# Unread products of a tile of ones at the ends and starts of the linear stages

## The reference, cut to what matters

```
def _rmsnorm(x, g):
    xf = x.astype(jnp.float32)
    y = xf * lax.rsqrt(jnp.mean(xf * xf, axis=-1, keepdims=True) + EPS)
    return (y * g.astype(jnp.float32)).astype(x.dtype)
...
        proj = _rmsnorm(h, norm_mix_g[l]) @ w_in[l]
...
        h = h + mixed @ w_out[l]
        h = h + _memory_attention(_rmsnorm(h, norm_mem_g[l]), ...)
        h = h + _peer_ffn(_rmsnorm(h, norm_peer_g[l]), ...)
...
    xn = rmsnorm(x, norm1_g)
    proj = xn @ w_in
...
    mixed = g_ssd * (y_ssd @ w_ssd_out) + g_mla * (y_mla @ w_mla_out) + g_gdn * (y_gdn @ w_gdn_out)
    h = x + mixed @ w_out
    f = jnp.square(jax.nn.relu(rmsnorm(h, norm2_g) @ w_up)) @ w_down
```

## Time and profile before

| | us |
|---|---|
| median of three timed runs | 5384.28 |
| lowest and highest of them | 5381.77, 5384.46 |
| profiled execution | 5380.81 |
| its span, first to last instruction | 5379.00 |
| PE busy in it | 5036.6 (94%) |
| DVE busy | 3028.1 (56%) |
| ACT busy | 1726.1 (32%) |
| POOL busy | 704.4 (13%) |
| mean granted TensorE clock | 0.959 |

### The profile page before, as it was taken

How to read it: one execution, slowest core, us unless ns; L and a number is a source line. 1 busy time by engine, 2 the same in 40 slices (tenths; PEclk the granted TensorE clock), 3 DMA queues, 4 the chain that set the end, 5 groups by cost and what they waited for, 6 DMA issues and landing times. The chain is left out here.

```text
span 5379.0 us, 61794 instructions
## 1 busy us (share of the span) xinstructions
PE 5036.6 (94%) x23862; PEld 4037.5 (75%) x23862; DVE 3028.1 (56%) x5431; ACT 1726.1 (32%) x2636; POOL 704.4 (13%) x493
## 2 busy tenths in 40 slices
PE   8778899999999999988899998999998999989998
PEld 6237678888878888877877686788778876767787
DVE  6577568899204444475555466544565555565433
ACT  3314333333322222232233323333322333323421
POOL 3741002222340000002200001100012000011000
PEclk9789999999999999989999998999989999989999
DMA  2012133555546555520022120222200221212222
GB/s 102 24 47 86 48 108 115 182 182 184 187 149 220 196 192 192 195 83 1 17 83 79 40 90 32 102 97 95 84 31 1 80 71 54 75 40 102 90 97 71
DMA packets 231730, 527.55 MB, mean 98 GB/s; under 512 B 19600, under 2 KB 89488, under 8 KB 230032
## 3 DMA queue, kind: packets, MB, share of 16 engines
q1 hardware_dynamic: 231440, 523.61, 28.8%
HBM read 448.03 MB, written 75.50 MB: 97 GB/s over the span
## 5 line engine op out<-in xcount | busy, mean ns | idle before, releaser
L408 DVE TENSOR_TENSOR weight_low<-ring,weight_high 128x1024 fp32r<-128x1024 f32 (+2 forms) x607 | 711.8, 1173 | 1269.5 <-PE banks L104 1204.1
L396 ACT CAST weight_high<-ring 128x1024 fp32r<-128x1024 f32 (+2 forms) x728 | 729.6, 1004 | 573.2 <-PE banks L104 552.4
L102 PE MATMUL banks<-x_high,weight_high 128*128 128x512 f32 x1856 | 752.9, 406 | 50.4 <-DVE x_low L461 22.9
L104 PE MATMUL banks<-x_high,weight_low 128*128 128x512 f32 x1856 | 732.9, 395 | 0.0
L103 PE MATMUL banks<-x_low,weight_high 128*128 128x512 f32 x1856 | 732.6, 395 | 0.0
L408 POOL TENSOR_TENSOR weight_low<-ring,weight_high 128x1024 fp32r<-128x1024 f32 (+1 forms) x121 | 300.0, 2481 | 2610.3 <-PEq L59 1621.6
L102 PEld LDWEIGHTS banks<-x_high,weight_high 128*128 128x128 f32 x1856 | 355.1, 191 | 163.9 <-issue 76.2
L103 PEld LDWEIGHTS banks<-x_low,weight_high 128*128 128x128 f32 x1856 | 354.8, 191 | 76.5 <-issue 5.8
L102 PE MATMUL banks<-xn_high,weight_high 128*128 128x512 f32 x1024 | 411.0, 401 | 0.7 <-ACT hT L1549 0.7
L104 PEld LDWEIGHTS banks<-x_high,weight_low 128*128 128x128 f32 x1856 | 354.0, 191 | 76.4
L102 PE MATMUL banks<-act_high,weight_high 128*128 128x512 f32 x1024 | 399.3, 390 | 11.1 <-DVE act_low L1760 11.1
(11 more groups left out here) (606 smaller groups left out, 9387.3 us busy)
## 6 DMA issues: line engine op xcount, KB each, us to landing
ring<-in_peer_u SPq DMA_DIRECT2D x128, 512.0 KB, 3.4
ring<-in_peer_v SPq DMA_DIRECT2D x128, 512.0 KB, 3.3
acts<-dot_act SPq DMA_DIRECT2D x128, 256.0 KB, 2.0
gates<-gate_block SPq DMA_DIRECT2D x64, 512.0 KB, 6.0
activations<-acts SPq DMA_DIRECT2D x128, 256.0 KB, 3.6
gates_in<-gates SPq DMA_DIRECT2D x128, 256.0 KB, 3.8
ring<-in_w_up SPq DMA_DIRECT2D x64, 512.0 KB, 3.3
ring<-in_w_down SPq DMA_DIRECT2D x64, 512.0 KB, 3.3
```

Source lines behind the costliest of these rows:

```text
L102: nc.tensor.matmul(out, w_high, x_high, start=start, stop=False)
L104: return nc.tensor.matmul(out, w_low, x_high, start=False, stop=stop)
L396: self.nc.scalar.copy(self.wH[:, g % HIGHS, 0:kc * P], self.ring[:, g % SLOTS, 0:kc * P]).then_inc(self.high_made, 1)
L408: ops.tensor_tensor(self.wL[:, g % LOWS, 0:kc * P], self.ring[:, g % SLOTS, 0:kc * P], self.wH[:, g % HIGHS, 0:kc * P].bitcast(F32), ALU.s ...
```

## The change

At the end of PE's stream of every `linears` stage it waits until the tile four back has been read, and then multiplies the tile of ones by itself nine times into that free bank. In stages with `fold` it does so five times into bank 0 ahead of the first tile. Nobody reads the results; the next product that uses the bank starts it anew.

```diff
+FILL_END, FILL_START = 9, 5
...
+        self.filler = None
+
+    def fill(self, bank, n):
+
+        for _ in range(n):
+            self.nc.tensor.matmul(bank[:, 0:P], self.filler, self.filler, start=True, stop=True)
...
             if pre:
                 pre.pe(eng)
+            if fold:
+                weights.fill(banks[0], FILL_START)
             for i, (sp, f) in enumerate(tiles):
...
                 for norm in norms:
                     norm.pe_at(eng, i)
+            last_read, f = tiles[total - SLOTS]
+            eng.wait_ge(last_read.bank_read, f + 1)
+            weights.fill(banks[total % SLOTS], FILL_END)
...
         weights = Weights(nc, held, ring)
         tools = (roots, eps, ident[:], columns, ones[:])
+        weights.filler = ones[:]
```

## The result

The changed kernel took 5351.62 us (median of four runs, 5346.58 to 5355.71), the kernel before beside it 5384.36. The ratio is 0.9944 with a 95% interval of 0.9931 to 0.9956: 0.56% faster, 33 us less. The forecast was 5357.0 us, 27.3 us less, in a range of 5346 to 5377.

The account below looks back on a forecast made before the run. TensorE was taken to lose time in short gaps and low-clock stretches behind them. Gains of 19.0, 10.2 and 0.6 less 2.5 us of costs made 27.3, from 5384.28 to 5357.0 us; range 5346 to 5377, the forecast's own 5348 to 5367.

Parts of the forecast that it names:

- The point at 0.28 us a product: At linears ends: above this price POOL's split no longer covers the nine; slower rival, 5405 to 5415 us, chance 0.06.
- Costs, 2.5 us: Stage ends the nine outlast: 0.6 us at each of two gdn_tail, 1.3 us at the last mlp.
- Class one: Nine low-clock stretches on first products of a following linears stage: 19.0 us back, 13 as lower bound.
- Class two: Eight low-clock stretches at starts of stages of another kind: 10.2 us back, bounds 4 and 21.4.
- (a): Start of choose, where its supposed transposes fill PE: 1.7 us back.
- (b): After both gdn_in, start to first gdn_acT: 2.8 us for both, half the full gain; bounds 0 and 5.6.
- (c): Rotations after mla_up, where DVE's chain waits only for the first product: 1.0 us each, 2.0 for both.
- (d): Stage after ssd_in, 0.29 us gained per us at the low level: 0.9 and 1.8 us in the two layers.
- (e): Turn of mem_v and the first scores after it: 1.0 us, bounds zero and 3.0.
- the ones do not hold the clock: Rival for all fills: products of ones count for nothing, gains are zero; 5387 to 5392 us, chance 0.09.
- Transposes earn no clock: Rival at stages opening with transposes: 5.4 us of gain fall away, 5362.4 us; chance 0.05.
- DVE takes it back: Rival in folded stages: DVE's weight split and squares set the third tile; 5 us gained, 5379 us; chance 0.08.

Follow-up runs that it names:

- e5: Changed kernel with eighteen instead of nine products of ones behind every linears stage; 5377.56 us, 0.9990 of the kernel before.
- e4: Changed kernel with products also behind rotations, attentions, delta-rule preparation and the stages after ssd_in, 18 behind gdn_in, fewer at some ends; 5333.39 us, 0.9908 of before.
- e6: Changed kernel with the nine only where another linears stage follows, the five in front kept; 5362.67 us, 0.9963 of the kernel before.
- e10: Changed kernel with the nine only where a stage of another kind follows, none in front; 5360.92 us, 0.9960 of the kernel before.
- e3: Changed kernel with every product of ones one column wide instead of 128; 5380.23 us, 0.9993 of the kernel before.
- e2: Changed kernel without the nine and their wait, only the five in front of folded stages; 5370.22 us, 0.9975 of the kernel before.
- e9: Changed kernel plus 13 products of ones behind the rotations' transposes in both layers; 5344.46 us in one run, no ratio.
- e1: Changed kernel with the nine at the ends only, the five in front left out; 5353.63 us, 0.9951 of the kernel before.

## Why the prediction was right

The time was forecast at 5357.0 and came at 5351.6, 5.4 us lower, inside the forecast's own range (5348 to 5367); the sign and the mechanism stand. Point by point:

- **The price.** 17 distances in 1.89 us are 0.111 a record, 0.222 a product, against 0.23. POOL covers the nine by 0.49 us; 0.4 was said. e5 bears out the size of the cover: eighteen overrun it by 1.5 us. The point at 0.28 us a product was met at no end of a `linears` stage; e4 only shows such products at a higher price elsewhere.
- **Costs, 2.5 us.** "gdn_tail" +0.55 and +0.60 (0.6 each), and at the last "mlp" the nine end 1.3 us after DVE's last addition. Right.
- **Class one, 19.0 us.** 17.4 in the stages and 1.3 of cost in one of them make 18.7; e6 shows the class by itself at 18.2 us timed. The 3.66 of layer 1's "mla_up" in it are not shown to be the products': e10, with none there, has 3.86, and e3 2.47. "mem_in" gives 1.57 of its 1.71 because DVE is just behind, as said: its split for the third tile is where it was (the first of the two in the row), and the weight load for the tile waits for it. Timeline after, to be read with the earlier trace rows:

```profile
487.06 2.55 DVE L415 TENSOR_TENSOR weight_low<-ring,weight_high 128x1024 fp32r<-128x1024 f32 x2
...
488.54 0.19 PEld L103 LDWEIGHTS banks<-mem_x_high,weight_high 128*128 128x128 f32 x1 [0.24 <-DVE weight_low L415]
488.57 0.80 PE L103 MATMUL banks<-mem_x_high,weight_high 128*128 128x512 f32 x1
```

- **Class two, 10.2 us.** 9.65 in the stages, by terms that miss in both directions. (a) 1.63 for 1.7. (b) after "gdn_in" 2.0 for 2.8: the rest of the gap was 2.64 us (2.6 said) and the clock did fall, for 3.4 us in layer 0 and 6.8 in layer 1; e5 with 18 has the full 2.8. (c) 1.9 for 2.0. (d) 1.6 for 2.7, of which 1.5 us go in the very next stage; and since e2, with nothing behind "ssd_in", and e3 have 0.9 and 1.9 there, the change's part in (d) isn't shown at all. (e) is the term that was mis-sized, 2.5 for 1.0: I had let ACT's copies hold back PE's first scores; in e3 the memory is at -0.01, in e10 at -3.07, the whole upper bound.
- **Layer 0's "gdn_in", 0.6 us.** 1.82 came, but e3 has 3.26 there. Not shown.
- **What the forecast had not.** It credited each saved stretch for good. "mem_out" (2.7) and the latent attention (4.2) gave 6.9 us back in the profile, and e9 shows the mechanism for layer 0's attention: a stage whose end DVE sets leaves TensorE a longer gap when TensorE gets faster. Gains of 8.1 us elsewhere, of the size that e3 shows without cause, stood against it. The sum came out right partly by that luck. The cause in "mem_out" stays open.
- **The starts.** I priced the five at nothing but the filling of a gap; e2 shows 13.9 us with them alone, some 7 of them in the folded starts by its profile, and none of my terms held those. What they add to the nine isn't settled.
- **The profile and the median.** The profiled executions differ by 25.1 us and the medians by 33 and 28. The one before was 3.6 us under its median and the one after 4.1 above it, which covers the difference to the first set.
- **The bound for a gap.** I took 1.7 us as kept and 2.84 as lost. That is no rule: the clock fell behind 2.48 us (e1) and behind waits of 1.21, 0.32 and 0.46 us, and it stayed behind 2.84 (e2), 3.40 (e10) and 3.34 us (e5).
- **Sums.** 36 and 17 us are not the bounds of the terms: those give 39.9 and 13.9, so 5344 to 5370. And both "gdn_in" ends and (e) at their upper bounds add 4.8 us to the gain, which gives 5352.2 and not 5345.
- **The transposes of "choose".** They are none; see the next paragraph. The price of (a) doesn't hang on it.

Of the rivals: *the ones do not hold the clock* is refuted by the windows after; e3 shows that it would have been true for narrower ones. *Transposes earn no clock* was argued from a misread line. Line 1500, with which "choose" opens, is the plain products of the queries with the keys; its records, unlike those of the transposes, have no `ident` among their inputs. So neither nor the -1.63 us of "choose" bears on transposes, and only (d) and (e) hung on this rival. Other rows do speak against it. Behind layer 0's "ssd_in" TensorE does nothing but transposes from 3251.93 to 3258.20, and the clock rises among them (before: timeline of PE, then windows of PE):

```profile
3251.93 3.47 PE L2097 MATMUL banks<-ident,ssd_xbc 128*128 128x128 f32 x16 [2.84 <-PEq L59]
3255.70 1.25 PE L2097 MATMUL banks<-ident,ssd_xbc 128*128 128x128 f32 x8 [0.30 <-DVE gdn_v L2133]
...
3251.48:3254.89 3.41, 2.96 (x13) 0.50 0.00 0
3254.89:3258.20 3.31, 2.82 (x21) 1.00 0.00 0
```

The Trainium skill, "TensorE: Matmul & The Clock Gate", Part 4, says that the full clock does not engage for transpose-mode matmuls; here it rose to 1.00 with transposes alone. Whether they run in the mode that the page means, the trace doesn't say.

*DVE takes it back* holds for 0.14 us of "mem_in" and not for the class.

## What to carry to other kernels

Where an engine is busy nearly everywhere and its granted clock still falls, look for the gaps in front of the low stretches, and fill them only as far as another engine's work covers them: nine products here gain 28 to 33 us, eighteen gain 3. Test such products against a version of them that should do nothing, and read several stages of it, since one profile's stages wander by 3 us and more. After such a change look again at the stages whose end another engine sets, since the faster engine now leaves a longer gap there.

## What the runs showed of the hardware

- Eighteen records of 128 columns took 2.17 us, eighteen of one column 2.06. The first kept the clock at the start of "mem_in", "peer_in", "choose" and layer 0's "mlp", the second didn't; behind both "mla_up" the second kept it too.
- The length of a gap does not decide alone. 2.84 us lost the clock in front of "choose" before and kept it in e2; 3.34 us in front of layer 1's latent attention lost it in after and kept it in e5; 3.40 us in front of layer 1's "mla_up" lost it before and kept it in e10. At the memory's end waits of 1.21, 0.32 and 0.46 us lost it in after and kept it in e10.
- The clock rose from 0.50 to 1.00 at 3254.89 of before, while TensorE had done nothing but transposes since 3251.93.
- The same kernel's stages differ between two executions by 1.0 to 2.8 us in the band attention, layer 1's state-space stage and layer 0's latent attention, while "mem_in", "peer_in", "choose", "ssd_in" and "mlp" repeat within 0.15 us; "mla_up" moved by 0.8 and 0.3. The runs of the kernel before lay between 5375.3 and 5389.3.
- Products meant to fill a gap cost more where the clock is low: 8.48 us for 48 records, 0.177 each, at a granted 0.65 in e4, against 0.111 each at 1.00.
